# FFN up-products: high and low features as one 512-column moving operand, with ScalarE copying the corrections out and VectorE adding them

## The reference, cut to what matters

```python
def conv_glu_ffn(h, w_up, conv_w, conv_b, w_down):
    a, u = jnp.split(h @ w_up, 2, axis=-1)
    a = lax.conv_general_dilated(a, conv_w[:, None, :], window_strides=(1,),
                                 padding=((CONV_WIDTH - 1, 0),),
                                 dimension_numbers=('NWC', 'WIO', 'NWC'),
                                 feature_group_count=D_FF) + conv_b
    return (jax.nn.silu(a) * u) @ w_down

def swiglu(h, w13, w2):
    a, b = jnp.split(h @ w13, 2, axis=-1)
    return (jax.nn.silu(a) * b) @ w2
```

## Time and profile before

| | us |
|---|---|
| median of 3 runs | 1892.18 (1892.04 to 1892.43) |
| the profiled execution | 1892.45 |
| its span | 1890.6 |
| TensorE matmuls busy | 1829.1 (97%) |
| TensorE weight loads busy | 1676.9 (89%) |
| VectorE busy | 1314.8 (70%) |
| ScalarE busy | 947.8 (50%) |
| GpSimd busy | 114.6 (6%) |
| mean granted clock of TensorE | 0.993 |

### The profile page before, as it was taken

One profiled execution on the slowest core, in us unless ns is written; L12 is line 12 of the kernel. 1 busy time (PEld: TensorE's weight loads), 2 busy tenths in 40 slices (PEclk: granted clock), 3 DMA queues, 4 the chain that ended last, 5 costly groups with the idle time before them and its releaser, 6 DMA issues.

```text
span 1890.6 us, 31038 instructions
## 1 busy us (share of the span) xinstructions
PE 1829.1 (97%) x12432; PEld 1676.9 (89%) x12432; DVE 1314.8 (70%) x2088; ACT 947.8 (50%) x1411; POOL 114.6 (6%) x158
## 2 busy tenths in 40 slices
PE   7999999999999999999998999999999999899997
PEld 6888999888899989999887889998999898789997
DVE  5576878747778887768766677677776776675545
ACT  5666444556654455344745354445434565454342
POOL 0000000000000000000004101100110001400100
...
DMA packets 67756, 376.98 MB, mean 199 GB/s; under 512 B 16000, under 2 KB 19712, under 8 KB 26048
## 3 DMA queue, kind: packets, MB, share of 16 engines
...
## 4 chain that ended last, share of the span: by engine, by line
PE 87%; DVE 7%; ACT 4%; issue 2%; DMA 0%; SPq 0%; DVEq 0%; ACTq 0%
PE bank L805 14%; PE bank L807 14%; PE bank L806 14%; PE bank L968 6%; PE bank L969 6%; PE bank L970 6%; PE bank L881 3%; PE bank L882 3%; PE bank L883 3%; DVE w_lo L2085 2%; PE bank L1448 1%; PE bank L931 1%; PE bank L932 1%; PE bank L933 1%; ACT w_hi L1546 1%
## 5 line engine op out<-in xcount | busy, mean ns | idle before, releaser
L2085 DVE TENSOR_TENSOR w_lo<-raw,w_hi 128x2048 fp32r<-128x2048 f32 (+4 forms) x279 | 605.8, 2175 | 76.4 <-ACT w_hi L1546 76.0
L805 PE MATMUL bank<-hT_hi,w_hi 128*128 128x256 f32 x2304 | 654.2, 284 | 2.0 <-DVE scratch L2826 2.0
L806 PE MATMUL bank<-hT_lo,w_hi 128*128 128x256 f32 x2304 | 651.9, 283 | 0.0
L807 PE MATMUL bank<-hT_hi,w_lo 128*128 128x256 f32 x2304 | 651.9, 283 | 0.0
L1546 ACT ACTIVATE w_hi<-raw 128x2048 fp32r<-128x2048 f32 (+4 forms) x268 | 502.1, 1875 | 147.4 <-PE bank L970 116.2
L805 PEld LDWEIGHTS bank<-hT_hi,w_hi 128*128 128x128 f32 x2304 | 440.2, 191 | 8.9 <-issue 6.5
L806 PEld LDWEIGHTS bank<-hT_lo,w_hi 128*128 128x128 f32 x2304 | 440.2, 191 | 2.8 <-issue 0.5
L807 PEld LDWEIGHTS bank<-hT_hi,w_lo 128*128 128x128 f32 x2304 | 440.2, 191 | 0.2
L968 PE MATMUL bank<-w_hi,hid_hi 128*128 128x512 f32 x528 | 206.9, 392 | 1.1 <-DVE hid_lo L2161 0.7
L969 PE MATMUL bank<-w_lo,hid_hi 128*128 128x512 f32 x528 | 206.3, 391 | 0.0
L970 PE MATMUL bank<-w_hi,hid_lo 128*128 128x512 f32 x528 | 205.5, 389 | 0.0
...
## 6 DMA issues: line engine op xcount, KB each, us to landing
...
```

The lines of the kernel that those rows point to most:

```text
L805: nc.tensor.matmul(out, ah, bh, start=(i == 0), stop=False)
L806: nc.tensor.matmul(out, ah, bl, start=False, stop=False)
L807: last = nc.tensor.matmul(out, al, bh, start=False, stop=(i == n - 1))
L2085: return nc.vector.tensor_tensor(w_lo[:, slot, cols], raw[:, raw_slot, cols], w_hi[:, slot, cols].bitcast(F32), ALU.subtract)
```

## The change

In all six FFNs the two matmuls that share the weights w_hi become one: hT_hi and hT_lo are two halves of one tensor hT, and hT[:, :, k, :], 2 x 256 columns, is the moving operand. Its product fills a bank: hi x hi in columns 0 to 255, the correction lo x w_hi in columns 256 to 511. The matmul with w_lo adds to the first half, as before. Each half of a tile (a, u) now has a bank of its own, so a tile takes two banks and the pair of tiles takes banks 0 to 3.

The correction is added afterwards. ScalarE copies both banks' second halves to upcorr (512 columns) and signals corr; VectorE adds them to both first halves into upsum (512 columns) and signals summed. ScalarE's first activation waits for summed. All that read the bank before (activation, taps, h32) read upsum in SBUF. TensorE's wait for a free bank is for summed instead of h. The order of k and halves is that of `feature_pair` in every tile.

The gate's product of the first FFN of a layer in the second stack moves from banks 2 and 3 to 4 and 5, and the first down chunk waits for its copies. To free semaphores, eight that the second mixer's gates use are merged into two (gate_pe, gate_act) that count through the same steps.

The program has fewer matmuls in the FFNs (32 for a tile instead of 48), one more activation and one more addition for each of 132 tiles.

```diff
-        hT_hi = sb("hT_hi", [P, KT, SEQ], F32R)
-        hT_lo = sb("hT_lo", [P, KT, SEQ], F32R)
+        hT = sb("hT", [P, 2, KT, SEQ], F32R)
+        hT_hi, hT_lo = hT[:, 0, :, :], hT[:, 1, :, :]
...
+        upsum = carve(2, 2, SEQ)
+        upcorr = carve(2, 2, SEQ)
...
-        UP, TP, ACC = ps[0:2], ps[2:6], ps[4:8]
+        UP, TP, ACC = [ps[0:2], ps[2:4]], ps[2:6], ps[4:8]
         TURN = [ps[2:4], ps[4:6]]
-        GATE = [ps[2:4], ps[0:2], ps[0:2]]
+        GATE = [ps[4:6], ps[0:2], ps[0:2]]
...
-        F = {n: sem("ffn_" + n) for n in ("y0", "sg", "h", "hid_hi", "hid_lo")}
+        F = {n: sem("ffn_" + n) for n in ("y0", "corr", "summed", "sg", "h", "hid_hi", "hid_lo")}
...
+            def up_pair(banks, slot, features=None):
+
+                for k in range(KT):
+                    if features:
+                        N, v = features
+                        pe.wait_ge(N["tp_lo"], split_in(v, 1, k) if N is A else split_at(v, k))
+                    for half in range(2):
+                        cols = slice((2 * k + half) * P, (2 * k + half + 1) * P)
+                        nc.tensor.matmul(banks[half].rearrange("p (w n) -> p w n", w=2), w_hi[:, slot, cols], hT[:, :, k, :],
+                                         start=(k == 0), stop=False, skip_group_check=True)
+                        last = nc.tensor.matmul(banks[half][:, 0:SEQ], w_lo[:, slot, cols], hT_hi[:, k, :],
+                                                start=False, stop=(k == KT - 1), skip_group_check=True)
+                return last
...
-                        pe.wait_ge(N["h"], f + (h0 - 1))
-                    if features:
-                        feature_pair(UP[f2], slot, features).then_inc(chunk_mm, 1)
-                        return
-                    feature_tile(UP[f2][:, 0:SEQ], slot, 0)
-                    feature_tile(UP[f2][:, SEQ:2 * SEQ], slot, 1).then_inc(chunk_mm, 1)
+                        pe.wait_ge(N["summed"], f + (h0 - 1))
+                    up_pair(UP[f2], slot, features).then_inc(chunk_mm, 1)
...
+                            if first and r == 0 and gate is not None:
+                                pe.wait_ge(B["gateb_ev"], due(B, "gateb_ev", 2 * gate + 2))
...
-                        pe.wait_ge(B["gcopy"], due(B, "gcopy", 1))
+                        pe.wait_ge(B["gate_act"], due(B, "gate_act", STEP["gcopy"]))
...
+                    nc.scalar.activation(upcorr[:, f2, :, :], psum[:, 2 * f2:2 * f2 + 2, SEQ:2 * SEQ], ACT.Copy).then_inc(N["corr"], 1)
+                    act.wait_ge(N["summed"], f + (h0 + 1))
                     if conv:
-                        nc.scalar.activation(cv[:, f2, :], UP[f2][:, 0:SEQ], ACT.Identity, scale=conv_tap(f, 2),
+                        nc.scalar.activation(cv[:, f2, :], upsum[:, f2, 0, :], ACT.Identity, scale=conv_tap(f, 2),
                                              bias=conv_tap(f, 3)).then_inc(N["c1"], 1)
                     else:
-                        nc.scalar.activation(sg[:, f2, :], UP[f2][:, 0:SEQ], ACT.Silu).then_inc(N["sg"], 1)
+                        nc.scalar.activation(sg[:, f2, :], upsum[:, f2, 0, :], ACT.Silu).then_inc(N["sg"], 1)
...
+                    dve.wait_ge(N["corr"], f + (h0 + 1))
+                    nc.vector.tensor_tensor(upsum[:, f2, :, :], psum[:, 2 * f2:2 * f2 + 2, 0:SEQ], upcorr[:, f2, :, :], ALU.add
+                                            ).then_inc(N["summed"], 1)
                     if conv:
                         dve.wait_ge(N["c1"], f + (h0 + 1))
-                        nc.vector.scalar_tensor_tensor(out=cv[:, f2, 1:SEQ], in0=UP[f2][:, 0:SEQ - 1], scalar=conv_tap(f, 1),
+                        nc.vector.scalar_tensor_tensor(out=cv[:, f2, 1:SEQ], in0=upsum[:, f2, 0, 0:SEQ - 1], scalar=conv_tap(f, 1),
                                                        in1=cv[:, f2, 1:SEQ], op0=ALU.mult, op1=ALU.add).then_inc(N["cv1"], 1)
                         dve.wait_ge(N["cv1"], f + (h0 + 1))
-                        nc.vector.scalar_tensor_tensor(out=cv[:, f2, 2:SEQ], in0=UP[f2][:, 0:SEQ - 2], scalar=conv_tap(f, 0),
+                        nc.vector.scalar_tensor_tensor(out=cv[:, f2, 2:SEQ], in0=upsum[:, f2, 0, 0:SEQ - 2], scalar=conv_tap(f, 0),
                                                        in1=cv[:, f2, 2:SEQ], op0=ALU.mult, op1=ALU.add).then_inc(N["cv2"], 1)
                     ahead()
                     dve.wait_ge(N["sg"], f + (h0 + 1))
-                    nc.vector.tensor_tensor(h32[:, f2, :], sg[:, f2, :], UP[f2][:, SEQ:2 * SEQ], ALU.mult).then_inc(N["h"], 1)
+                    nc.vector.tensor_tensor(h32[:, f2, :], sg[:, f2, :], upsum[:, f2, 1, :], ALU.mult).then_inc(N["h"], 1)
```

47 lines of the change are left out of this document (23 added, 24 removed), and 2 rows, old and new, of the table B.

## The result

The changed kernel takes **1925.72 us** (median of four) against 1892.18: a ratio of 1.018 (95% interval 1.016 to 1.019), 33.5 us slower. Three of the four lie between 1924.55 and 1925.85; the fourth took 2992.4 at a mean granted clock of 0.556 and is left out of the ratio. The forecast was 1910.5 with a range to 1921: the sign and the place were right, and the size was short by 15 us. The span of the profiled execution is 1924.0 us.

What follows compares the result with a forecast made beforehand. TensorE bounds the kernel now; VectorE was to bound the two convolution FFNs. Their +27.6 us and the four others' -9.3 make +18.3 on the profiled 1892.45, 1910.5 us after allowing for the median; range 1900 to 1921.

Steps and rivals of the forecast that it cites:

- VectorE's own sequence: FFNs with convolution: VectorE's operations and waits in series, two tiles, a third split, three modulation products, 18.07 us a half-turn.
- TensorE's gain: Up-products: a third of the matmuls dropped, columns kept; 0.20 us less a tile, 4.4 an FFN, 26.6 for six.
- the sum 0.228 + 0.120: Up-products, per k and half: one 512-column and one 256-column matmul take 0.348 us instead of 3 x 0.120 = 0.360.
- The rival for a lower gain: Up-products: a dropped matmul is worth little, 0.04 us a tile, four other FFNs gain 0.9 each; 1925; chance 8%.
- Two hand-overs at 0.92 and 0.73: Convolution FFNs' loop, each tile: sum's start to activation 0.92 us, activation to first convolution step 0.73, in series.
- half-turn 18.07: Convolution FFNs: two feature tiles up, one down chunk, three weight chunks split; 18.07 us instead of 16.98.
- VectorE becomes the bound: Convolution FFNs: VectorE's half-turn 18.07 us against TensorE's 16.58; plus 13.8 us for each such FFN.
- 2.0 us as the point of decision: VectorE's half-turn, convolution FFNs: below 2.0 us added, TensorE stays the bound; forecast adds 3.5. Rival that cover holds: 10%.
- it takes VectorE's pace: TensorE in convolution FFNs: each up-product and down chunk needs a w_lo split in VectorE's sequence, so TensorE waits for it.
- Tail stalls: End of the four FFNs without convolution: TensorE stalls 0.3 or 1.4 us for chunk 32, 1.5 or 0.4 for last tile.
- The rest, at nothing: Earlier bank release, the gate's move to banks 4 and 5, merged semaphores and the DMA queue: no effect on time.

Runs made afterwards that it cites:

- e1: Changed kernel with high and low features side by side for each k, a moving operand of 512 consecutive columns: 1924.4 us, 1.017 of the kernel before.
- e2: Changed kernel with, for each k, both halves' 512-column matmuls first, then both 256-column ones: 1916.6 us, 1.013 of the kernel before.
- e7: Changed kernel with matmul widths in pairs within one bank (512-column ones of k and k+1, then their 256-column ones): 1916.1 us, 1.013 of the kernel before.
- e8: Changed kernel with widths alternating, each 256-column matmul following a 512-column one of the other bank: 1922.3 us, 1.016 of the kernel before.
- e5: Changed kernel with VectorE's modulation products in the two convolution FFNs 64 columns wide instead of 1,024: 1917.0 us, 1.013 of the kernel before.
- e9: Changed kernel with VectorE's weight split ahead of its wait for the first convolution step, convolution FFNs only: 1906.2 us, 1.008 of the kernel before.
- e10: e9 with three more 256-column VectorE operations ahead of each sum in the convolution FFNs: 1949.7 us, 1.030 of the kernel before.
- e13: e9 with e5's small products, both in the convolution FFNs only: 1893.9 us, 1.001 of the kernel before.
- e6: Changed kernel with, in each FFN's last turn, the next stage's chunk split and VectorE's last modulation product moved later: 1921.1 us, 1.015 of the kernel before.
- e11: Changed kernel with three 256-column matmuls in convolution FFNs and every FFN's last two tiles, the rest 512 + 256 ordered by width: 1878.9 us, 0.994 of before.
- e12: e11 with the 512 + 256 form in all six FFNs except their last two tiles, and e9's early split: 1884.5 us, 0.996 of the kernel before.
- e14: e12 with convolution FFNs' modulation products of tile steps moved into VectorE's wait for the second activation: 1877.4 us, 0.993 of the kernel before.
- e3: Changed kernel without ScalarE's copy and VectorE's sum, later steps reading the banks' first halves (512 + 256-column matmuls alone): 1879.9 us, 0.993 of the kernel before.

## Why a pair of matmuls gained half as much

In the changed kernel, TensorE in an FFN without convolution: a 512-column matmul, then a 256-column one.

```profile
1199.81 0.40 PE L947 MATMUL bank<-hT,w_hi 128*128 128x512 f32 x1
1200.05 0.28 PE L949 MATMUL bank<-hT,w_lo 128*128 128x256 f32 x1
1200.17 0.40 PE L947 MATMUL bank<-hT,w_hi 128*128 128x512 f32 x1
1200.40 0.28 PE L949 MATMUL bank<-hT,w_lo 128*128 128x256 f32 x1
1200.52 0.40 PE L947 MATMUL bank<-hT,w_hi 128*128 128x512 f32 x1
...
1201.93 0.40 PE L947 MATMUL bank<-hT,w_hi 128*128 128x512 f32 x1
```

Six pairs from 1199.81 to 1201.93 are 2.12: 0.353 each, where the earlier trace rows made 0.348 of 0.228 and 0.120. Of the 12 ns that a pair was to gain on 0.360, 7 are there and 5 are missing. Four kernels ask where they went.

**e1, one piece.**

```
-  hT = sb("hT", [P, 2, KT, SEQ], F32R)
+  hT = sb("hT", [P, KT, 2, SEQ], F32R)
-  ... w_hi[:, slot, cols], hT[:, :, k, :], ...
+  ... w_hi[:, slot, cols], hT[:, k, :, :], ...
```

> The high and low features stand side by side for each k (moving operand of 512 consecutive columns in place of two pieces of 256 that lie 2,048 elements apart); nothing else is changed. Measured in the changed kernel: a pair of 512 and 256 columns is spaced 0.353 us where 0.348 was forecast, so a tile gains 0.11 us and not 0.20. Theory 1, the two-piece operand costs the missing 5 ns: pairs spaced 0.348, each FFN without convolution 1.8 us shorter than in the changed kernel, those with it unchanged (VectorE sets their pace), 1925.7 - 7 = 1918.5. Theory 2, the 5 ns come with the change of width from 512 to 256 and back: spacing stays 0.353, 1925.7. Theory 3: the time lies in the 512-column matmul whatever its operand's layout; 1925.7 too, and the order by width tells it from theory 2.

Measured 1924.4 and spacing 0.353: the operand's two pieces cost nothing.

**e2, by width.** For each k first the 512-column matmuls of both halves, then both 256-column ones (wide and narrow stand for the two matmuls of `up_pair`):

```
-  for half in range(2):
-      wide(half, k); narrow(half, k)
+  for half in range(2):
+      wide(half, k)
+  for half in range(2):
+      narrow(half, k)
```

> Same matmuls as the changed kernel, in another order: for each k both 512-column ones first, then both 256-column ones (the banks are written in turn). Theory 2, a change of width costs: half as many changes, so two pairs take 0.701 in place of 0.706, an FFN without convolution is 0.9 us shorter, 1925.7 - 4 = 1922. Theory 3, the 512-column matmul itself costs more than the 0.228 of a down-product's: 512 after 512 spaced 0.235 or more, two pairs 0.706, 1925.7. Writing two banks in turn could also cost; then the 256-column ones would be spaced over 0.120.

Measured 1916.6, 9 less than the changed kernel where 4 were expected. Its timeline on TensorE (x2 stands for two matmuls in one row):

```profile
1196.13 0.62 PE L947 MATMUL bank<-hT,w_hi 128*128 128x512 f32 x2
1196.59 0.40 PE L950 MATMUL bank<-hT,w_lo 128*128 128x256 f32 x2
1196.83 0.63 PE L947 MATMUL bank<-hT,w_hi 128*128 128x512 f32 x2
...
1198.91 0.63 PE L947 MATMUL bank<-hT,w_hi 128*128 128x512 f32 x2
```

Four steps from 1196.13 to 1198.91 are 2.78, 0.348 for each pair: the forecast's sum. F3 to F6 get 1.8 to 2.0 shorter than in the changed kernel. But in e2 the banks changed too, so two more kernels tell bank from width.

**e7, one bank, widths in pairs.**

```
-  for k in range(KT):
-      for half in range(2):
-          wide(half, k); narrow(half, k)
+  for k in range(0, KT, 2):
+      for half in range(2):
+          wide(half, k); wide(half, k + 1); narrow(half, k); narrow(half, k + 1)
```

> The changed matmuls with widths in pairs, but one bank four times in a row: for one half the 512-column ones of k and k+1, then their 256-column ones (the first tile in the changed kernel's order). The run that ordered by width had both banks in turn, and its two pairs took 0.696 in place of 0.706. Theory, it is the change of width that costs: 0.696 here too, an FFN without convolution 1.8 us shorter than in the changed kernel, 1925.7 - 7 = 1918.5. Rival, it is the 256-column matmul that adds to the bank that the 512-column one just before it has written: three of four matmuls here follow one in the same bank but only one pair in two is a 512 followed by a 256; 0.701, 1922. If the bank counts whatever the width: 0.706, 1925.7.

Measured 1916.1, and F3 to F6 as in e2.

**e8, widths in turn, other bank.**

```
+  wide(0, 0)
   for k in range(KT):
-      wide(0, k); narrow(0, k); wide(1, k); narrow(1, k)
+      wide(1, k); narrow(0, k); wide(0, k + 1) if k < KT - 1; narrow(1, k)
```

> The other half of that question: widths alternate (512, 256, 512, 256) but each 256-column matmul follows a 512-column one of the other bank (the first tile in the changed kernel's order). Theory, change of width costs: spacing of a pair stays 0.353, 1925.7. Rival, the same bank costs: 0.348, 1918.5.

Measured 1922.3; a tile's 16 pairs take 5.52 from first to last matmul, 5.53 in the changed kernel and 5.46 in e2. So it is neither layout nor bank: **widths that change at every matmul cost 5 ns a pair, and widths in twos cost nothing**. The price isn't one per change, since with half as many changes all of it was gone. What in TensorE makes it isn't shown.

## What sets the pace of the convolution's FFNs

The forecast named VectorE's own sequence, 18.07 long. Taking work from it is the direct trial.

**e5, small products.** In the convolution's FFNs:

```
-  w = w[:, half * DM:(half + 1) * DM]
+  w = w[:, half * DM:half * DM + 64]
-  ... in0=w, scalar=1.0, in1=cb, ...
+  ... in0=w, scalar=1.0, in1=cb[:, 0:64], ...
```

> The changed kernel with VectorE's modulation products in the two convolution FFNs 64 columns wide instead of 1,024 (the rest of each product is left out of the result). That takes some 0.95 us off each of the three in a half-turn. Theory, VectorE's sequence sets the pace there: 18.15 less 2.85 is 15.3, under TensorE's 16.79, so the half-turn falls to 16.79, VectorE waits and TensorE doesn't; the two FFNs shrink from +16.6 and +18.5 to -2.1 plus the tail's waits (some 0.3 and 2.4), about +0.6 each: 1925.7 - 34 = 1892. Rival, the two hand-overs between ScalarE and VectorE are what costs, whatever else VectorE does: half-turns stay near 18, 1920 or more. Rival, ScalarE is late as well: half-turns between 17 and 18, 1900 to 1912.

Measured 1917.0: with 2.9 us less work for VectorE in each half-turn, it fell from 18.15 to 18.0. My theory had this wrong. VectorE is now idle for 2.75 us ahead of a sum, where it is never idle for more than 0.07 in the loop of the changed kernel. I followed who waits for whom. From e5's timeline of TensorE, the waits ahead of two up-products that follow a down-product, one half-turn apart:

```profile
264.25 0.50 PE L947 MATMUL bank<-hT,w_hi 128*128 128x512 f32 x1 [0.57 <-DVE w_lo L2102]
...
282.31 0.49 PE L947 MATMUL bank<-hT,w_hi 128*128 128x512 f32 x1 [0.68 <-DVE w_lo L2102]
```

ScalarE between them, the copy of the tile that TensorE began at 264.25:

```profile
270.20 0.60 ACT L1618 ACTIVATE scratch<-bank 128x512 f32<-128x512 f32 x1 [3.41 <-PE bank L949]
```

VectorE, that tile's sum, the next tile's sum, and the next tile's weight split:

```profile
270.83 0.69 DVE L2168 TENSOR_TENSOR scratch<-bank,scratch 128x512 f32<-128x512 f32 x1 [2.75 <-ACT scratch L1618]
...
277.17 0.69 DVE L2168 TENSOR_TENSOR scratch<-bank,scratch 128x512 f32<-128x512 f32 x1
...
279.89 2.28 DVE L2102 TENSOR_TENSOR w_lo<-raw,w_hi 128x2048 fp32r<-128x2048 f32 x1
```

This is a closed chain. Up-product A starts at 264.25; 5.95 later ScalarE copies; 0.63 later A's sum; 6.34 later, behind all of A's steps, B's sum; 2.72 later, behind B's two convolution steps, the weight split; and 2.42 later the next up-product A, which needs that split. 5.95 + 0.63 + 6.34 + 2.72 + 2.42 = **18.06**. (The pieces add up to the measured half-turn by themselves; what makes them a chain is that each starts on the end of the one before.) So a second limit, made mostly of latencies, lay 0.1 to 0.2 under the first: in the changed kernel VectorE's products end at 271.40, where the chain alone would have let the sum start at 270.60 (the start of ScalarE's copy there) + 0.63 = 271.23.

**e9, split early.** VectorE's split (`ahead()`) moves ahead of its wait for the first convolution step, in the convolution's FFNs:

```
   if conv:
+      ahead()
       dve.wait_ge(N["c1"], f + (h0 + 1))
...
-  ahead()
+  if not conv:
+      ahead()
   dve.wait_ge(N["sg"], f + (h0 + 1))
```

> One move in the changed kernel: in the two convolution FFNs VectorE's weight split stands ahead of its wait for ScalarE's first convolution step instead of behind the second step. No work is taken away. New theory after the run with small products (2.85 us less work for VectorE in a half-turn, and the half-turn fell by 0.15 alone): two limits lie side by side. One is VectorE's sequence, 18.15. The other is a chain through the engines: up-product A 5.95, copy 0.62, A's whole post on VectorE 6.34, B's sum to its split 2.72, split to TensorE 2.42, together 18.05, and only then can the next up-product A start. The move shortens both: the split covers the 1.0 us wait for ScalarE, so a tile holds VectorE 5.1, its half-turn is 2 x 5.1 + 0.2 + 2.20 + 3.45 = 16.0, and the chain is 5.95 + 0.6 + 5.3 + 0.7 + 2.4 = 15.0. TensorE's 16.79 is left as the bound: minus 2.1 for each such FFN, plus tail waits of some 1.4 and 2.5, so about +1.8 each in place of +16.6 and +18.5: 1925.7 - 31.5 = 1894. Rival, VectorE's or ScalarE's work itself is too much: half-turns stay at 18, no change, 1925. Rival, the split ahead delays the convolution and with it hid_lo, and the down-product waits instead: 17 to 18.

Measured 1906.2. One line moved and no work taken away gives back 19.5 us, 18.7 of it in these two FFNs, about half of what the change had lost there. The move shortens the chain and VectorE's sequence alike, so this run alone doesn't tell the two apart. Half-turns are 17.08, not 16.79. Its VectorE shows why:

```profile
272.10 0.69 DVE L2168 TENSOR_TENSOR scratch<-bank,scratch 128x512 f32<-128x512 f32 x1
272.70 2.28 DVE L2102 TENSOR_TENSOR w_lo<-raw,w_hi 128x2048 fp32r<-128x2048 f32 x1
274.90 0.48 DVE L2173 SCALAR_TENSOR_TENSOR scratch<-scratch,spa 128x255 f32<-128x255 f32 x1
275.52 0.48 DVE L2176 SCALAR_TENSOR_TENSOR scratch<-scratch,spa 128x254 f32<-128x254 f32 x1
276.49 0.42 DVE L2181 TENSOR_TENSOR scratch<-scratch 128x256 f32<-128x256 f32 x1 [0.48 <-ACT scratch L1628]
277.40 0.42 DVE L2183 TENSOR_TENSOR hid_lo<-scratch,hid_hi 128x256 fp32r<-128x256 f32 x1 [0.48 <-ACT hid_hi L1630]
```

The 1.0 us wait for the first convolution step is covered, but behind the second step VectorE now waits 0.48 for the second activation (L1628), which the split used to cover. A tile holds it 5.64 (272.10 to 277.74, its next operation) and not my 5.1: 5.64 + 5.80 (the first tile, with 0.15 to the next sum) + 2.20 + 3.45 = 17.09.

**e10, split early with load.** e9, and ahead of each tile's sum in the convolution's FFNs:

```
+  for spare in (h32, cv, sg):
+      nc.vector.tensor_tensor(spare[:, f2, :], psum[:, 2 * f2, 0:SEQ], upcorr[:, f2, 0, :], ALU.add)
```

> The run before this one (split early) with three more VectorE operations of 256 columns ahead of each sum in the convolution's FFNs (results unused), some 0.38 each, 1.15 a tile. It tells the two limits apart with the chain short: VectorE's sequence would be 16.0 + 2.3 = 18.3, the chain 15.0 + 2.3 = 17.3, TensorE 16.79. Theory, both limits are real: half-turns of 18.3, VectorE without gaps, and each of the two FFNs about +16: 1922. Rival, the chain alone was the limit in the changed kernel and VectorE's sum is not: half-turns of 17.3, +7 each, 1904.

Measured 1949.7. The three take 1.00 together, and half-turns are 19.07, 1.99 over e9's 17.08: every added microsecond shows. The load lies in the chain as well, so the sum alone doesn't decide; but in the loops of e9 and e10 VectorE never stands more than 0.07 us ahead of a tile's first operation, where a chain that bound would leave it idle, as in e5. With the chain short, **VectorE's sequence is a limit of its own**.

**e13, both.** e9 with e5's small products.

> Small products (64 of 1,024 columns, the rest left out of the result) and the split ahead of the wait for the first convolution step, both in the convolution's FFNs only. If the chain from an up-product through its tile's posts to the split was the second limit at 18.0, it is now some 15, VectorE's sequence 17.09 - 2.85 = 14.2, and TensorE's 16.79 is left: half-turns of 16.79, each of the two FFNs from +8.2 (split early) to about +2.5 with its tail waits, 1895. If something else held the small-products run at 18.0 (ScalarE's order, a transfer), half-turns stay at 17 or above: 1903 to 1920.

Measured 1893.9 (1895 expected), looped half-turns of 16.74 to 16.81. Neither step alone reaches TensorE's pace: less work gives 18.0, where the chain binds; the early split gives 17.09, where the sequence binds; both give 16.79. That is what two limits side by side look like, and it settles the cause of the longer half-turns.

## The tail

**e6, tail.** On ScalarE and on VectorE, in every FFN:

```
-  post(FT - 1, 1, 1, FFN_N - 3, next_first)
+  post(FT - 1, 1, 1, FFN_N - 3, lambda: None)
+  next_first()
...
-  for k in ((0,), (1,), (2, 3), (4,), () if conv else (5,))[q] if end ...
+  for k in ((0,), (1,), (2, 3), (4,), ())[q] if end ...
...
   post(FT - 1, 1, 1, lambda: None)
-  if conv:
+  if conv or full == turns:
       ada(turns - 1, 5)
```

> The changed kernel with two moves in the last turn of every FFN: ScalarE splits the next stage's chunk behind the last tile's hid_hi instead of ahead of it, and VectorE's last modulation product stands behind the last tile instead of ahead of the split of chunk 32. Theory: the tail's waits in the four other FFNs (1.2 and 1.3 us in the first of them) go, and each FFN gains 2.1 against before as in the run of the matmuls alone: +0.7, +0.6, -0.4, -1.4 become about -1.9 each, 7 together. In the convolution's FFNs the last hid_lo comes some 1.1 earlier and the wait before it falls from 2.4 to 1.3; if that long wait is what makes the clock fall to half, the 1.7 us of slow matmuls go too: 2.8 each. Sum 1925.7 - 7 - 5.6 = 1913; if the clock falls all the same, 1916.5. Rival, the next stage's chunk is then late and the stage behind waits: 2 us given back per FFN.

Measured 1921.1, where 1913 to 1916.5 was expected. In the changed kernel TensorE waits in F3's tail as forecast, for chunk 32 and for the last tile:

```profile
918.84 0.50 PE L981 MATMUL bank<-w_hi,hid_hi 128*128 128x512 f32 x1 [1.18 <-DVE w_lo L2102]
...
922.46 0.50 PE L981 MATMUL bank<-w_hi,hid_hi 128*128 128x512 f32 x1 [1.26 <-DVE hid_lo L2181]
```

In e6 both are gone and F3 and F4 end 2.1 and 2.3 sooner, F5 1.0 sooner. But outside the FFNs e6 loses what it had gained there: +3.3 where the changed kernel has -1.2. From F4's end to F5's start, for one, it takes 7.40 instead of 6.17, with 2.4 instead of 1.2 of waits on TensorE, and behind F3 TensorE waits 0.58 and 0.45 for x where the changed kernel shows a single 0.25. The rival was right in kind, a late next chunk is paid for in the next stage; not all of the 4.5 is traced. C1 and C2 got 1.7 and 2.1 shorter, where 1.1 was expected from the earlier hid_lo and 1.7 more if the clock held.

## A version that is faster than both

**e11, mixed for four.** Both lessons, and no second hand-over where nothing covers it: the convolution's FFNs and the last two tiles of each FFN go by three 256-column matmuls read from the banks; the rest by 512 + 256 columns ordered by width.

```
+  def paired(f, conv):
+      return f < FT - 2 and not conv
   (up_pair, the two posts and the bank's wait follow it)
```

> A version meant to be faster than both: the convolution's FFNs and the last two tiles of every FFN by three 256-column matmuls, read from the banks as before (two banks a tile stay); the other 20 tiles of the four other FFNs by 512 + 256 columns with copy and sum, ordered by width. No waits in the tails (the last tiles have no second hand-over), and a pair of widths at 0.348: 20 x 16 x 0.012 = 3.8 us for each of four FFNs, 15.4, and 1.2 outside: 1892.2 - 16.6 = 1875.6. If the width order's gain is lost where plain tiles mix in, 1884; if the tail still waits, 1880.

Measured 1878.9, 0.994 of before (0.993 to 0.996). C1 and C2 are as before, F3 to F6 gain 3.5 to 3.8 (3.8 expected). Most of what is missing to the expected 1875.6 lies outside the FFNs: +0.7 where -1.2 was counted on.

**e12, mixed for six**, with e9's split early for the paired tiles:

```
   def paired(f, conv):
-      return f < FT - 2 and not conv
+      return f < FT - 2
```

> The same for all six FFNs, with the weight split early in the convolution's: if the split early frees TensorE there, each of those two gains 3.8 as well (their last two tiles are plain too, so no tail waits): 1892.2 - 6 x 3.8 - 1.2 = 1868. If the convolution's half-turns stay at VectorE's pace, 1900 or more. If their tail waits 1 to 2 us each for VectorE, 1871.

Measured 1884.5: the convolution's half-turns stay at VectorE's 17.09, and the forecast written before e9 was known missed them.

**e14, mixed for six, filled.** In VectorE's `post`, for the convolution's FFNs (and no product behind a tile's hid_lo there):

```
+  meanwhile()      # the product that stood behind the tile
   dve.wait_ge(N["sg"], f + (h0 + 1))
```

> The mixed version for all six FFNs (1884.5) with the modulation products of tile steps in the convolution's FFNs moved from behind the tile's hid_lo into VectorE's wait for the second activation. One such product a half-turn covers 0.48 of waiting: VectorE's 17.09 becomes 16.6, about TensorE's own 16.6 with widths in pairs. Each of the two FFNs gets 8 x 0.45 = 3.6 shorter (+4.3 and +3.9 become +0.7 and +0.3): 1877.3, level with the mixed version for four FFNs (1878.9) within what can be told. If the wait isn't filled but moved behind the product, 1884.

Measured 1877.4 (1877.3 expected), 0.993 of before (0.991 to 0.994), half-turns of 16.58 to 16.59. That the sum came out to 0.1 is in part luck: C1 and C2 are -0.9 and -1.3 where +0.7 and +0.3 were expected, the stretches outside 1.1 longer than in e12, and e12's profiled execution lies 1.6 above the median that the sum started from. In its VectorE timeline the product stands where the 0.48 was:

```profile
272.72 0.48 DVE L2201 SCALAR_TENSOR_TENSOR scratch<-scratch,spa 128x254 f32<-128x254 f32 x1
273.12 1.22 DVE L2117 SCALAR_TENSOR_TENSOR scratch<-scratch 128x1024 f32<-128x1024 f32 x1
274.26 0.08 DVE L2117 DVE_READ_ACCUMULATOR scratch<-scratch  x1
274.26 0.42 DVE L2207 TENSOR_TENSOR scratch<-scratch 128x256 f32<-128x256 f32 x1
```

C1 and C2 still don't gain the 3.8 of the other four. In the last turn of C1 TensorE waits 1.11 and 1.78 for w_lo, behind a VectorE that has stood 2.11 for a modulation product's data (in C2 0.73 and 1.77, behind 1.24); how much of these waits the transfer makes isn't shown.

e11 and e14 can't be told apart, and both beat the kernel before by 0.6 to 0.7%.

## Why the prediction was right in its place and short in its size

The forecast of +18.3 stands against +33.4 in the profile. By its own steps:

- **TensorE's gain was mis-sized.** 0.20 a tile, 4.4 an FFN; measured 2.1 (e3). In the four other FFNs that is 4 x 2.3 = 9.2 of the missing 15.1. The step that failed is the sum 0.228 + 0.120, each read from a run of equal matmuls and put together for a mixed run; with widths in twos (e2, e7) the sum holds. A slip of arithmetic adds to it: (0.360 - 0.348) x 16 is 0.19 a tile and 4.2 an FFN, not 0.20 and 4.4, so 0.2 of each 2.3 is rounding. The rival for a lower gain had the right direction, but not the reason, and that its 1925 lies next to the result is luck: it had 14 us less gain, of which 9.2 came, and the other 6 came from terms that it didn't have. By the rule of the Trainium skill behind that rival (TensorE: Matmul & The Clock Gate, Back-to-back issue gap), which the page gives for an isolated matmul, a dropped matmul would be worth 0.04 us a tile. Here the trace doesn't agree: measured is 0.10 to 0.11 with the widths alternating and 0.19 (F5 and F6 of e11: 3.8 over 20 tiles) with them in twos.
- **Two hand-overs at 0.92 and 0.73, half-turn 18.07: right.** Measured 0.92 (sum at 271.40, ScalarE's start at 272.32) and 0.78 (to 273.10), and half-turns of 18.13 to 18.18; of the 0.20 of waiting forecast ahead of the second sum 0.06 is there. Over eight half-turns and the last turn that is 1.2 us more than forecast in each of C1 and C2.
- **"VectorE becomes the bound", with 2.0 us as the point of decision: half right.** It is one of two limits that happened to lie within 0.2 us of each other. The number came out right because both did; by the forecast's reasoning e5 had to give 1892 and gave 1917. I had followed TensorE's need of w_lo only as "it takes VectorE's pace", not as a loop with a length of its own.
- **Tail stalls: right.** Forecast 2.9, 2.9, 1.8 and 0.7 for F3 to F6; measured, as what lies above -2.1, 2.8, 2.7, 1.7 and 0.7.
- **A TensorE clock at its lower level, 1.2 GHz, after the last wait of C1 and C2: missing from the forecast.** The sweep behind the last hid_lo takes 10.34 instead of 8.79 and 9.46 instead of 7.91: 1.55 each, 3.1 together.
- **C2 takes 1.9 more than C1 over and above: missing.** 0.8 of it stands in its last turn, where VectorE waits for the transfer of a modulation product's data, which the forecast took to be there in time; what causes the other 1.1 isn't known (both below).
- **"The rest, at nothing": right**, -1.2.

Sum: 9.2 - 0.3 (tails) + 2 x 1.2 + 3.1 + 1.9 - 1.2 = 15.1. The range ended 10.5 above the forecast. It left out the rival with the low gain, at 8% and 1925; for the spacing of a mixed run the text had both bounds, no gain and 0.22 a tile, and then took the value next to the upper one because a run of equal matmuls gave it. For the clock, for a late transfer and for a second limit there was no term.
